# A triangular inversion on packed 32x32 blocks, and the experts' end in another order

## The reference, cut to what matters

```python
def step(state, inp):                       # RWKV-7, 256 steps, 8 heads of width 64
    r_t, d_t, k_t, v_t, kk_t, a_t = inp
    sa = jnp.einsum('bhij,bhj->bhi', state, -kk_t)
    state = (state * d_t[:, :, None, :] + sa[..., None] * (kk_t * a_t)[:, :, None, :]
             + v_t[..., None] * k_t[:, :, None, :])
    return state, jnp.einsum('bhij,bhj->bhi', state, r_t)

hdn = jax.nn.gelu(jnp.einsum('cd,chkd->chk', xc, uc).astype(jnp.float32), approximate=False) * gc
return jnp.einsum('chk,chkd->cd', hdn.astype(vc.dtype), vc)      # PEER: experts' sum, by token
h = h + gt2 * peer_ffn(xn2, peer_wq[l], peer_subkeys[l], peer_u[l], peer_v[l])
```

## Time and profile before

| | us |
|---|---|
| median of 3 runs | 1643.19 (1643.02 to 1643.37) |
| the profiled execution's own time | 1643.05 |
| its span, first to last instruction | 1641.2 |
| TensorE busy in the span | 1600.5 (98%) |
| VectorE, ScalarE, GpSimd busy | 1264.6, 868.8, 194.6 |
| inversion, 182.10 to 213.72 us | 31.62 |
| the four chunks, 215.35 to 238.60 us | 23.25 |

### The profile page before, as it was taken

The page is one execution under the profiler, slowest core; times in us unless marked ns, Lnnn a source line. Parts: engine busy times, 40 slices in busy tenths (PEclk is TensorE's granted clock), DMA queues, the critical chain, the costliest instruction groups (busy, mean ns, idle before and its releaser), DMA issues.

```text
span 1641.2 us, 32821 instructions
## 1 busy us (share of the span) xinstructions
PE 1600.5 (98%) x11530; PEld 1420.1 (87%) x11530; DVE 1264.6 (77%) x2681; ACT 868.8 (53%) x1598; POOL 194.6 (12%) x153
## 2 busy tenths in 40 slices
PE   6999999999999999999999999999999999999998
PEld 4887988899988878888888888888899877999998
DVE  6885548859989988788878888888778455688887
ACT  3444221364469944555555555555654245566665
POOL 0020211017700000000000000000048003300000
PEclk9999999999999999999999999999999999999999
DMA  9742136855741278777777777777545561255553
GB/s 356 292 145 87 35 118 225 332 187 176 226 133 62 94 260 265 235 238 236 234 239 235 237 243 233 242 235 236 187 158 172 198 208 40 76 171 185 184 179 128
DMA packets 102625, 316.92 MB, mean 193 GB/s; under 512 B 11392, under 2 KB 21376, under 8 KB 102144
## 3 DMA queue, kind: packets, MB, share of 16 engines
q1 hardware_dynamic: 101664, 311.27, 56.6%
q10 hardware_dynamic: 864, 4.32, 0.7%
HBM read 309.65 MB, written 5.90 MB: 192 GB/s over the span
## 4 chain that ended last, share of the span: by engine, by line
PE 79%; DVE 7%; ACT 6%; POOL 2%; issue 2%; DMA 2%; SPq 1%; DVEq 0%; POOLq 0%; ACTq 0%
PE bank L515 10%; PE bank L502 9%; PE bank L503 8%; PE bank L504 8%; PE bank L2106 7%; PE bank L2108 7%; PE bank L2110 7%; PE bank L523 5%; POOL wlo L496 2%; ACT arena L2069 2%; PE bank L1624 2%; PE bank L1742 2%; ACT arena L2060 2%; PE bank L763 2%; PE bank L1325 1%
## 5 line engine op out<-in xcount | busy, mean ns | idle before, releaser
L491 ACT CAST whi<-wring 128x1024 fp32r<-128x1024 f32 x395 | 412.7, 1046 | 179.3 <-PE bank L504 109.9
L496 DVE TENSOR_TENSOR wlo<-wring,whi 128x1024 fp32r<-128x1024 f32 x341 | 416.9, 1224 | 62.7 <-ACT whi L491 53.7
L496 POOL TENSOR_TENSOR wlo<-wring,whi 128x1024 fp32r<-128x1024 f32 x54 | 138.0, 2562 | 910.8 <-ACT whi L491 910.7
L502 PE MATMUL bank<-xboth,whi 128*128 128x256 f32 x752 | 219.2, 292 | 6.8 <-POOL wlo L496 2.6
L503 PE MATMUL bank<-xboth,whi 128*128 128x256 f32 x752 | 212.6, 283 | 0.0
L504 PE MATMUL bank<-xboth,wlo 128*128 128x256 f32 x752 | 212.5, 283 | 0.0
L515 PE MATMUL bank<-xboth,whi 128*128 128x512 f32 x704 | 188.7, 390 | 0.0
L2106 PE MATMUL bank<-whi,Whi 128*128 128x512 f32 x512 | 159.9, 393 | 2.6 <-DVE Wlo L2222 2.6
L2108 PE MATMUL bank<-wlo,Whi 128*128 128x512 f32 x512 | 158.5, 391 | 0.0
L2110 PE MATMUL bank<-whi,Wlo 128*128 128x512 f32 x512 | 157.7, 389 | 0.0
L502 PEld LDWEIGHTS bank<-xboth,whi 128*128 128x128 f32 x752 | 143.9, 191 | 13.5 <-issue 6.4
(11 more groups left out here) (396 smaller groups left out, 3115.1 us busy)
## 6 DMA issues: line engine op xcount, KB each, us to landing
wring<-in_w SPq DMA_DIRECT2D x463, 512.0 KB, 3.9
arena<-in_ada SPq DMA_DIRECT2D x48, 512.0 KB, 7.6
xn<-in_ada SPq DMA_DIRECT2D x96, 256.0 KB, 2.8
h_spill<-arena SPq DMA_DIRECT2D x37, 128.0 KB, 2.2
arena<-h_spill SPq DMA_DIRECT2D x37, 128.0 KB, 3.9
wring<-in_w SPq DMA_DIRECT2D x6, 384.0 KB, 4.5
wring<-in_w SPq DMA_DIRECT2D x8, 256.0 KB, 3.0
arena<-in_const ACTq DMA_DIRECT2D x1, 1151.0 KB, 5.2
```

The source lines that it names most:

```text
L491: act.copy(whi[:, n % HSLOTS, :], wring[:, n % SLOTS, :]).then_inc(hi_ready, 1)
L496: eng.tensor_tensor(wlo[:, n % SLOTS, :], wring[:, n % SLOTS, :], whi[:, n % HSLOTS, :].bitcast(F32), ALU.subtract).then_inc(lo_ready, 1)
L502: pe.matmul(out, h, xh, start=start, stop=False, **kw)
```

## The change

The inversion works on the two 32x32 diagonal blocks of each 64x64 matrix, packed: partition strip 64r + 32b holds block b of head r, and a unit column is 32 wide instead of 64. `tiles` replaces `blocks64`: for a unit column four matmuls of 32x32 with 32 moving columns, one on each of the four diagonal strips of the array. Four levels (b = 1 at the start, then 2, 4, 8, 16) are done so; that is 8 + 8 + 8 = 24 calls. The last level touches only the lower left 32x32 block, which is one product L T and one product with `TTm` for each unit, 32 matmuls each, on two strips at a time; ScalarE and VectorE copy the first result out (L1411 of the changed kernel on ScalarE), and then the blocks into the full `TTc`. The start values are computed from two extra products (64 matmuls each, 64 rows by 32 columns) ahead of and among the units' matrices, in place of L1616, by four VectorE operations instead of eight. Increments of `Tm` for both halves now come before those of the transpose. The filler moves: 4 steps ahead of the inversion instead of 12, 8 more behind the chunks. In the experts' end, block 0 is copied by ScalarE while TensorE is on block 1, block 1 is copied by both engines, the transposes go by block, ScalarE's table load comes behind its copies, and in the last turn VectorE's split of the next weights comes behind the sum that the GELU waits for.

```diff
-CONST1 = [("g_mask", 256), ("mL", 6 * 64), ("mT1", 64), ("id64", 64), ("causal", 384), ("rot_moba", 128)]
+CONST1 = [("g_mask", 256), ("mL", 5 * 32), ("mT1", 32), ("id32", 32), ("causal", 384), ("rot_moba", 128)]
...
+        tile32 = lambda r, b: slice(64 * r + 32 * b, 64 * r + 32 * b + 32)
+        TILES32 = [(r, b) for r in range(2) for b in range(2)]
...
-            act_gates1(act, 6, 8)
+            act_gates1(act, 6, 7)
+            act.wait_ge(t_new, 8)
+            act.wait_ge(t_x, 11)
+            act.copy(Xm[tile32(1, 1)], sixteen(bank[4][tile32(1, 1), 0:512])).then_inc(t_xm, 1)
+            for r, b in TILES32:
+                act.copy(TTc[tile32(r, b), :, 32 * b:32 * b + 32], TTm[tile32(r, b)]).then_inc(t_new, 1)
+            act_gates1(act, 7, 8)
             act_gate_hi(act, 10)
-            act_gates1(act, 8, 9)
-            act.wait_ge(t_new, 10)
...
+            dve.wait_ge(t_x, 1)
+            v.then(dve.tensor_tensor(Tm, sixteen(bank[7][:, :]), over(level(0), UN), ALU.mult))
+            dve.tensor_tensor(Tm, Tm, over(c1["id32"], UN), ALU.add).then_inc(t_init, 1)
...
+            dve.wait_ge(t_x, 11)
+            dve.tensor_copy(Xm[tile32(0, 1)], sixteen(bank[4][tile32(0, 1), 0:512])).then_inc(t_xm, 1)
+            dve.wait_ge(tt_inc, 9)
+            for r in range(2):
+                dve.tensor_copy(TTc[tile32(r, 0), :, 32:64], sixteen(bank[6][tile32(r, 0), 0:512])).then_inc(t_new, 1)
...
-        AT_UNITS, AT_PRODUCTS, AT_CHUNKS = 49, 61, 73
+        AT_UNITS, AT_PRODUCTS, AT_CHUNKS = 49, 53, 65
...
+            for u in range(UN):
+                for r, b in TILES32:
+                    s = slice(32 * b, 32 * b + 32)
+                    mm = pe.matmul(bank[7][tile32(r, b), 32 * u:32 * u + 32], ARc[rows64[r], u, 0, s],
+                                   BKc[rows64[r], 0, u, s], start=True, stop=True)
+            mm.then_inc(t_x, 1)
...
-            def blocks64(bk, n, left, right):
+            def tiles(out, n, left, right):
 
                 for i in range(8):
                     u = 8 * (n % 2) + i
-                    for r in (lo, hi):
-                        mm = pe.matmul(bk[r, 64 * i:64 * i + 64], left[r, u, :], right[r, u, :], start=True, stop=True)
+                    for r, b in TILES32:
+                        rows = tile32(r, b)
+                        mm = pe.matmul(out[rows, 32 * i:32 * i + 32], left(u, r, b), right[rows, u, :],
+                                       start=True, stop=True)
                 return mm
...
+            pe.wait_ge(t_added, 8)
+            for u in range(UN):
+                for r in range(2):
+                    mm = pe.matmul(bank[4][tile32(r, 1), 32 * u:32 * u + 32], LT[tile32(r, 0), u, 32:64],
+                                   Tm[tile32(r, 0), u, :], start=True, stop=True)
+            mm.then_inc(t_x, 1)
+            pe_gates1(pe, AT_PRODUCTS + 6, AT_PRODUCTS + 8)
+            pe.wait_ge(t_xm, 10)
+            pe.wait_ge(t_new, 8)
...
+                if c == 0:
+                    pe.wait_ge(t_new, 14)
...
-            pe.wait_ge(tok_ready, 2)
-            for m in range(KT):
-                for b in range(TT):
+            for b in range(TT):
+                pe.wait_ge(tok_ready, 2 * b + 1)
+                for m in range(KT):
...
+            act.wait_ge(tok_pe, 1)
+            for f in range(2):
+                ins = act.copy(tok[:, 0, f * 512:(f + 1) * 512], tok_accs[0][f][:, :])
+            ins.then_inc(tok_ready, 1)
+            act.wait_ge(tile_done, P0 + COUNT["peer"])
+            act.copy(tok[:, 1, 512:1024], tok_accs[1][1][:, :]).then_inc(tok_ready, 1)
             act_table(act, ACT.Sqrt)
...
                 n, b = u_tile(j), j % 3
-                lo(n + 2, i)
+                if j < NK - 1:
+                    lo(n + 2, i)
                 dve.wait_ge(h_rest, 3 * i + (j - EARLY + 1))
                 dve.tensor_tensor(ge[:, b, :], bank[j % 3][:, 0:S], ge[:, b, :], ALU.add).then_inc(h_summed, 1)
+                if j == NK - 1:
+                    lo(n + 2, i)
```

More of the change, by code:

```diff
@@ L128, in shape_constants @@
     strict, incl = same & (p < f), same & (p <= f)
-    level = [(p // (2 * b) == f // (2 * b)) & (p // b % 2 == 1) & (f // b % 2 == 0) for b in (1, 2, 4, 8, 16, 32)]
+    level = [(p // (2 * b) == f // (2 * b)) & (p // b % 2 == 1) & (f // b % 2 == 0) for b in (1, 2, 4, 8, 16)]
     q = np.arange(128)[:, None]
@@ L150, in shape_constants @@
     both = lambda m: np.tile(m[:64, :64], (2, 1))
-    one = [*(both(m) for m in (strict, incl, strict, incl)), *(both(m) for m in level), both(level[0].T), both(np.eye(128)), causal, rotation(MD, MD // 8),
+    fourfold = lambda m: np.tile(m[:32, :32], (4, 1))
+    one = [*(both(m) for m in (strict, incl, strict, incl)), *(fourfold(m) for m in level), fourfold(level[0].T), fourfold(np.eye(128)), causal, rotation(MD, MD // 8),
            sum_pair, give_pair]
@@ L1413, in act_rwkv @@
                 act.copy(yv[:, :, c, :], quarters(bank[6 + c % 2])).then_inc(q_yc, 1)
[L1414 to L1417, removed]
+                if c == 2:
+                    act_gate_hi(act, 11)
+            act_gates1(act, 9, 10)
+            act_gate_hi(act, 12)
         def dve_rwkv(dve, v):
@@ L1463, in dve_rwkv @@
                                   ALU.mult).then_inc(u_masked, 1)
[L1464 to L1473, removed]
+                if p == 2:
+                    dve.wait_ge(t_x, 2)
+                    v.then(dve.tensor_tensor(TTm, sixteen(bank[7][:, :]), over(c1["mT1"], UN), ALU.mult))
+                    dve.tensor_tensor(TTm, TTm, over(c1["id32"], UN), ALU.add).then_inc(t_init, 1)
+            dve.wait_ge(t_init, 2)
             def masked(n):
@@ L1477, in masked, with add_inc, add_tt_inc @@
                 s = slice(8 * (n % 2), 8 * (n % 2) + 8)
-                dve.tensor_tensor(Xm[:, s, :], eight(bank[4 - n % 2]), over(level(1 + n // 2), 8), ALU.mult).then_inc(t_xm, 1)
-            def update(n):
+                dve.tensor_tensor(Xm[:, s, :], eight(bank[4 - n % 2][:, 0:256]), over(level(1 + n // 2), 8),
+                                  ALU.mult).then_inc(t_xm, 1)
+            def add_inc(n):
+                s = slice(8 * (n % 2), 8 * (n % 2) + 8)
+                if n >= 2:
+                    dve.wait_ge(t_added, n - 1)
+                dve.wait_ge(t_inc, n + 1)
+                dve.tensor_tensor(Tm[:, s, :], Tm[:, s, :], eight(bank[4 - n % 2][:, 0:256]), ALU.add).then_inc(t_added, 1)
+            def add_tt_inc(n):
                 s = slice(8 * (n % 2), 8 * (n % 2) + 8)
@@ L1629, in product, with increment @@
                     pe.wait_ge(t_added, n - 1)
-                blocks64(bank[4 - n % 2], n, LT, Tm).then_inc(t_x, 1)
-            def increments(n):
+                tiles(bank[4 - n % 2], n, lambda u, r, b: LT[tile32(r, b), u, 32 * b:32 * b + 32], Tm).then_inc(t_x, 1)
+            def increment(n):
                 pe.wait_ge(t_xm, n + 1)
@@ L1635, in increments, with tt_increment @@
                     pe.wait_ge(t_new, n - 1)
[L1636 to L1640, removed]
+                tiles(bank[4 - n % 2], n, lambda u, r, b: TTm[tile32(r, b), u, :],
+                      Xm).then_inc(t_inc, 1)
+            def tt_increment(n):
+                tiles(bank[6 + n % 2], n, lambda u, r, b: Xm[tile32(r, b), u, :], TTm).then_inc(tt_inc, 1)
             pe_gates1(pe, AT_UNITS, AT_PRODUCTS)
@@ L1726, in act_rwkv_out @@
             act.activation(rB["crow"], rB["crow"], ACT.Silu).then_inc(crow_ready, 1)
-            for t in range(11, COUNT["gates1"]):
+            for t in range(10, COUNT["gates1"]):
                 act_gates1(act, t, t + 1)
@@ L2110, in down_tokens @@
                     mm = pe.matmul(tok_accs[b][f][:, :], Wl, h[:, f * 512:(f + 1) * 512], start=False, stop=last)
+                if last and b == 0:
+                    mm.then_inc(tok_pe, 1)
             return mm
```

87 lines of the change are left out of this document (44 added, 43 removed).

## The result

The changed kernel takes 1665.35 us (median of 4 runs, 1663.91 to 1666.66) against 1643.28 for the kernel before (4 runs, 1643.02 to 1644.16): a ratio of 1.0132, with a 95% interval from 1.0121 to 1.0144. 1632.8 was predicted. The profiled execution took 1666.66, its span is 1664.9.

The account below looks back on a forecast made before the run. TensorE, busy 98%, was taken as the bound, the inversion lasting as long as its instructions. -13.5 + 2.0 + 0.3 + 0.5 + 0.2 + 0.6 - 0.5 = -10.4 from 1643.05 gave 1632.65, median 1632.8; range 1629.5 to 1636 us.

Parts of the forecast that it names:

- 24 calls of `tiles` at 0.50 us (12.0 us): Inversion: each call, 16 steps of half length on strips four deep, takes 0.50 us, near the 0.46 of exact halving.
- the 31 ns of a record: TensorE's time per record in the old inversion (7.92 us for 256), taken to be spent on moving columns, not instructions.
- 12.0 + 2.0 + 0.3: Inversion: 24 calls 12.0 us, hand-overs staying at 2.0, and 0.3 of TensorE waiting for the first mask in level 1.
- The start values: Ahead of the inversion: L1616 (2.03 us) goes, two products of 64 matmuls take 2.5 in all, +0.5; bounds 0 and +2.
- The last level: End of the inversion: two products, two strips deep, 1.0 us each, 2.0 together, with 0.3 of waiting between; bounds 0 and 1.
- paid by the instruction: Rival, chance 0.04: a record costs 31 ns whatever its columns, 1920 new records cost 59.5 us, result 1675.5.
- its point of decision: Threshold in the instruction rival: from 14 ns a record on, over 1920 records, the change is slower.
- Paid back in waits: Rival, chance 0.13: calls take 0.5 us, but slower 256-column PSUM operations and uncovered hand-overs cost 4.0; result 1636.8.
- two deep: Rival, chance 0.15: four strips share what two share now, an inversion call costs 0.91 us again; 1643.9, no change.
- the moved gate steps: Eight filler steps moved behind the chunks: same work, 0 in sum, giving back 3 us of the earlier gain there.
- the direction of the experts' end: Reordered copies, transposes, table load and last turn after the experts: together -0.5 us; bounds -1.0 and 0.
- two of the signs that were to show the forecast wrong: Among the listed signs: one call's records spaced 14 ns or more on average; granted clock below full in the inversion.

Follow-up runs that it names:

- no_start2: Changed kernel without its second set of start products, transposed start values taken from masked Gram blocks by VectorE: 1662.52 us, 2.8 less.
- after_rep8: Changed kernel with its first inversion call (64 records) made nine times instead of once: 1677.29 us, 11.9 over the changed kernel.
- filler16: Changed kernel with 16 more gate steps brought forward into the inversion: 1659.86 us, 5.5 under the changed kernel.
- bf16_inc: Changed kernel with both operands of the increments held as bf16, one record per matmul instead of two: 1650.51 us, 14.8 less.
- wide128: Changed kernel with each `tiles` matmul moving up to 128 columns instead of 32, by the same instructions: 1664.3 us, not told from the changed kernel.

## Why the prediction was wrong

**The step that failed** is "24 calls of `tiles` at 0.50 us (12.0 us)", and before it the choice of what the 31 ns of a record are: "if on moving columns, half the columns cost half; if on instructions, twice as many cost twice". The rows on which I chose columns show that strips run side by side, and they do: 9 to 10 ns a record in a burst at full clock, 13 at half. But those rows are groups of 2, 4 and 16 records, and each fits many times into one packet of 128. They speak for a burst and say nothing of 1536 records in a row. The 24 calls with the filler between them were to take about 17 us (12.0 + 2.0 + 0.3, and six steps of 0.41) and took 43.64: 27 of the 35 us by which the lag at the first chunk misses the forecast (-13.5, with the eight moved steps, against +21.72).

**The start values** were put at 2.5 us for both sets. The first is as predicted, 1.25 (lag +1.27 at the first unit). With the second the lag rises by 7.15: 2.40 of "issue" around L1626, 1.50 of its own records, and about 3 of units at half clock behind the gap (L1638 x8 takes 0.85 there and 0.44 elsewhere). So a gap costs beyond the calls, in the work behind it. Taking that set out (no_start2) brought the units' end 5.3 us forward, and VectorE's start values, then in the chain, took 2.9 of that back.

**The last level**, L1690 and L1698, took 1.53 and 1.85 where 1.0 each was taken. The granted clock from 229.30 to 235.00 us, where they lie, is 0.50.

**The rival "paid by the instruction"** had the right mechanism in name and a chance of 0.04. Its price, 31 ns, gave 1675.5; at 28.4 ns by its own sum 1920 records cost 54.5 and the time is 1670.5, 5 us too much: the first set of start products took 1.27 where 128 records at 28.4 ns are 3.6, six gate steps ran within the packets' time, and the experts' end gave 1.0 for its 0.5; this is not added up further. The mean lies above its point of decision, 14 ns a record, and I excluded it by the start times of neighbours. The figure by the Trainium skill's page on TensorE ("TensorE: Matmul & The Clock Gate", Wait — 56ns, not 53.3ns?), 1664, came within 1.4 us by luck: starts in a burst are closer than 25 ns (9 to 13), and only the mean over the stretch, 28.4, is not.

**"Paid back in waits" and "two deep"** are both refuted: the first by after_rep8, whose repeated calls have no waits, the second by the bursts, where a call takes 0.55 to 0.65 at full clock and not 0.91.

**Right:** the moved gate steps (22.3 to 25.2, 2.9 us against "3"), the calls within a burst, the direction of the experts' end (though alone it is not told from nothing), and two of the signs that were to show the forecast wrong, records spaced 14 ns and more on average and a clock below full.

The packets' size agrees with the Trainium skill ("Runtime: NRT & Kernel Launch", Instruction fetch mechanics), which says that an engine's instructions come in 16 KiB blocks over a queue of its sequencer's, and that crossing a block is mostly hidden. The second half does not hold here: at 3.64 us a packet, 1 to 2.5 us of most of them was idle.

## What to carry to other kernels

Before splitting a matmul into smaller ones, count the records and not only the columns: at 3.5 to 3.7 us for 128 loads and matmuls, a record costs some 28 ns over a long row, and a float32 matmul of two records 56, however short the bursts. Read the idle time that is put down to "issue" and the packets of the instruction queue beside it, and test a price on as many instructions in a row as the change will issue. Where such a stretch can't be avoided, use fewer records per matmul (bf16 operands here), or write long matmuls that have to be done anyway into it, since they run almost for nothing (16 gate steps for 0.5 us in filler16).

## What was not expected of the hardware

- TensorE's instructions came in packets of 16 KB, 128 load and matmul pairs each, no faster than one in 3.45 to 3.72 us when they were wanted at once, with the DMA engines nearly idle (16 GB/s from 184 to 230 us). The packets themselves are short: 72 took 0.3% of 16 engines' 1664.9 us, about 1.1 us each. From 185 to 196 us a packet begins about 1 us behind the start of a burst, and the next burst starts 2.4 to 3.2 us behind the packet's start, so some 1.5 us behind its end (an estimate from these). What fills that time, and whether other traffic lengthens it, was not tried.
- A float32 matmul is two records of load and matmul, one of bf16 operands is one: 544 fewer for the edit of bf16_inc (12490 to 11946).
- The granted clock fell to 0.50 behind gaps of about 2 us; with gaps of 0.4 to 0.7 (wide128, from 180 us on) it stayed at 1.00.
